# A two-layer fp32 decoder trunk on one core: the steps from each norm to the next matmuls in another order and in smaller pieces

## What is computed

```python
h = adaLN(RMSNorm(x), c)          # silu(c) @ ada_w + ada_b gives scale, shift and gate
x = x + gate1(c) * (hybrid_mixer(h) @ w_out)
h = adaLN(RMSNorm(x), c)
scores = sigmoid(h @ router_w); sel = scores + router_bias
grp_score = top_k(sel.reshape(ntok, 4, 4), 2)[0].sum(-1)   # sum of the two best of a group
best = argmax(grp_score)
for e in range(16):
    out += combine[:, e] * ((silu(h @ w_gate[e]) * (h @ w_up[e])) @ w_down[e])
x = x + gate2(c) * out
```

## Time and profile before

| | |
|---|---|
| median of 3 runs | 1483.7 us (1481.28 to 1484.05) |
| the profiled execution, its own time | 1478.49 us |
| its span in the profile | 1476.7 us |
| PE busy | 1408.2 us, 95% |
| DVE busy | 1159.0 us, 78% |
| ACT busy | 786.3 us, 53% |

### The profile page before, as it was taken

One profiled execution on the slowest core, in us unless ns is written; L12 is line 12 of the kernel. 1 busy time (PEld: TensorE's weight loads), 2 busy tenths in 40 slices (PEclk: granted clock), 3 DMA queues, 4 the chain that ended last, 5 costly groups with the idle time before them and its releaser, 6 DMA issues.

```text
span 1476.7 us, 19233 instructions
## 1 busy us (share of the span) xinstructions
PE 1408.2 (95%) x7638; PEld 1137.8 (77%) x7638; DVE 1159.0 (78%) x1344; ACT 786.3 (53%) x756; POOL 106.7 (7%) x180
## 2 busy tenths in 40 slices
PE   3999899999899999999989989999999999999998
PEld 3889777788799977766569877778879998776654
DVE  6589689865688878888875987898757856799886
...
DMA packets 174777, 357.46 MB, mean 242 GB/s; under 512 B 12316, under 2 KB 18704, under 8 KB 173664
## 3 DMA queue, kind: packets, MB, share of 16 engines
...
## 4 chain that ended last, share of the span: by engine, by line
PE 82%; DVE 9%; ACT 6%; issue 2%; DMA 1%; SPq 0%; DVEq 0%; ACTq 0%
PE bank L632 24%; PE bank L634 24%; PE bank L633 24%; DVE w_low L1718 4%; PE bank L1138 1%; PE bank L712 1%; DMA ring<-in_ada_w 1%; PE bank L596 1%; ACT w_high_zu L1240 1%; PE bank L760 1%; PE bank L807 1%; DVE scratch L2289 1%; PE bank L857 1%; PE bank L1035 1%; ACT w_high_xbc_sc L1217 1%
## 5 line engine op out<-in xcount | busy, mean ns | idle before, releaser
L634 PE MATMUL bank<-h_high,w_low 128*128 128x256 f32 x864 | 243.8, 282 | 0.0
L1718 DVE TENSOR_TENSOR w_low<-ring,w_high_qk_score 128x2048 fp32r<-128x2048 f32 x72 | 164.8, 2288 | 39.3 <-ACT w_high_qk_score L1217 21.3
L1718 DVE TENSOR_TENSOR w_low<-ring,w_high_zu 128x2048 fp32r<-128x2048 f32 x66 | 151.1, 2289 | 46.4 <-ACT w_high_zu L1240 26.4
L633 PE MATMUL bank<-w_low,h_high 128*128 128x512 f32 (+2 forms) x480 | 183.7, 383 | 0.0
L1718 DVE TENSOR_TENSOR w_low<-ring,w_high_xbc_sc 128x2048 fp32r<-128x2048 f32 x68 | 155.6, 2289 | 29.4 <-ACT w_high_xbc_sc L1217 27.1
L634 PEld LDWEIGHTS bank<-h_high,w_low 128*128 128x128 f32 x864 | 163.7, 189 | 0.0
L633 PE MATMUL bank<-w_low,rows_high 128*128 128x512 f32 (+2 forms) x384 | 151.6, 395 | 0.0
L1217 ACT ACTIVATE w_high_zu<-ring 128x2048 fp32r<-128x2048 f32 x50 | 95.6, 1911 | 69.9 <-PE bank L634 66.0
L1217 ACT ACTIVATE w_high_xbc_sc<-ring 128x2048 fp32r<-128x2048 f32 x50 | 95.6, 1912 | 62.0 <-PE bank L634 58.5
L1217 ACT ACTIVATE w_high_qk_score<-ring 128x2048 fp32r<-128x2048 f32 x52 | 99.5, 1913 | 32.4 <-PE bank L634 29.1
L633 PEld LDWEIGHTS bank<-w_low,h_high 128*128 128x128 f32 x480 | 91.5, 191 | 18.9 <-issue 1.9
...
## 6 DMA issues: line engine op xcount, KB each, us to landing
...
```

The costliest lines, as they stand in the source:

```text
L633: mm(out_, lh, rl, start=False, stop=False, skip_group_check=True)
L634: return mm(out_, ll, rh, start=False, stop=stop, skip_group_check=True)
L1718: V.tensor_tensor(w_low[:, slot, :, cols], ring[:, slot, :, cols], high[:, :, cols], ALU.subtract).then_inc(w_split, 1)
```

## The change

**Start of layer 0.** The two reciprocals and the scaling of tile 1 stand ahead of the seventh weighing. The last weighing is done in two column halves (`weigh_last`), and PE turns each half into columns as it is there. The fills ahead of the transposes are 4 instead of 8; the 5 ahead of the columns and the 8 behind them are replaced by 5 behind them. Unit 0 is rounded and split in two halves of the contraction (`start_rounded`, `start_split`), one ahead of the columns and one behind DVE's first modulation.

**Start of both layers.** The channel blocks are modulated in pairs: ACT takes blocks 0, 1 and 4, 5, DVE 2, 3 and 6, 7, and rounding and splitting go by the same pairs; the first projection waits pair by pair. In layer 1 two fills are added behind the transposes.

**Second norm to first expert, both layers.** Tile 0's modulation on DVE is cut in three blocks ahead of the last `add_output` and one behind; its rounding and splitting by halves; `xn_high` and `xn_low` by tile (`round_normed`, `split_normed`), the first tile's rounding inside the norm, the second's behind the sigmoid, the second's split behind the choice of groups. The sum of the two best of four is taken as the largest of two sums of pairs and one sum of the larger ones. Fills ahead of the counts are 3 instead of 6. Of the gathered rows, 4 and 6 on ACT and 5 and 7 on DVE are taken behind the pieces of the first expert unit.

The diff, cut to its core:

```diff
...
-            pe.wait_ge(sums_ready, layer + 1)
+            if layer > 0:
+                pe.wait_ge(sums_ready, layer + 1)
             for n in range(ADA_0):
+                if layer == 0 and n % 2 == 0:
+                    pe.wait_ge(first_columns, n // 2 + 1)
                 c0 = (MOE_CHUNKS - ADA_0 + n) * W
                 last = chunk_columns(bank[:, 3, :], PROWS + 4 * n, ada_sums[:, c0:c0 + W])
             last.then_inc(columns_in, 1)
...
             pe.wait_ge(first_used, 5)
-            busy(8)
+            busy(4)
         pe.wait_ge(xn_ready, l * 6 + 2)
         modulate_transposes(1)
         if l == 0:
-            pe.wait_ge(first_used, KD - 1)
+            layer_columns(0)
             busy(5)
-            layer_columns(0)
-            busy(8)
             pe.wait_ge(pcol_ready, 2)
+        else:
+            busy(2)
         b = begin("proj", "C")
         for h in range(2):
-            pe.wait_ge(h_split, l * 2 + h + 1)
             w = split_unit()
-            tok_project([b[:, 0, t * 256:t * 256 + 256] for t in range(TT)], w, h, 0, 256, h_early, True)
+            for k in (0, 2):
+                pe.wait_ge(h_split, l * 4 + 2 * h + k // 2 + 1)
+                tok_project([b[:, 0, t * 256:t * 256 + 256] for t in range(TT)], w, h, 0, 256, h_early, True,
+                            ks=range(k, k + 2))
             chan_project(b[:, 1:2, :], w, h, 256, range(2), h_early).then_inc(units_read, 1)
...
         b = begin("v", "count")
-        busy(6)
+        busy(3)
...
+            take_rows(4)
+            take_rows(6)
...
         def first_modulate():
+            def columns(b, k0):
+                for k in range(2):
+                    last = A(hT[:, k0 + k, :], b[:, k * SEQ:k * SEQ + SEQ], ACT.Identity,
+                             scale=modc[:, 0, 0, k0 + k:k0 + k + 1], bias=modc[:, 0, 1, k0 + k:k0 + k + 1])
+                last.then_inc(h_even, 1)
+            def rounded(k0):
+                A(h_high[:, k0:k0 + 2, :], hT[:, k0:k0 + 2, :], ACT.Copy).then_inc(h_rounded, 1)
             act.wait_ge(modc_ready, l * 2 + 1)
...
+            columns(job("s", "h1_0"), 0)
+            act.wait_ge(h_even, l * 2 + 1)
+            rounded(0)
+            act.wait_ge(h_odd, l * 2 + 1)
+            act.sem_inc(s_evac, 2)
+            seen["s"] += 1
+            rounded(2)
+            act.wait_ge(v_ready, l * NVR + V_PLAIN.index("h1_2") + 1)
+            columns(ps("h1_2"), 4)
+            act.wait_ge(h_even, l * 2 + 2)
+            rounded(4)
+            act.wait_ge(h_odd, l * 2 + 2)
+            act.sem_inc(v_evac, 2)
+            rounded(6)
+        def round_normed(t):
+            act.wait_ge(xn_ready, l * 6 + 4 + 2 * t)
+            A(xn_high[:, t, :], merged[:, t, :], ACT.Copy).then_inc(xn_rounded, 1)
...
-            round_mixer(0)
+            act.wait_ge(slot_loaded[0], 16 * LANDED[0])
+            for k in (0, 2):
+                A(mixer_high[0][:, k:k + 2, :], ring[:, 0, k:k + 2, :], ACT.Copy).then_inc(
+                    w_rounded if k else start_rounded, 1)
         first_modulate()
...
         second_square(0, 1)
         second_norm(0)
+        round_normed(0)
         second_square(1, 0)
         second_modulate(0)
+        act.wait_ge(s_evac, l * NSJ + S_JOBS.index("h2_0") + 1 + 2)
+        A(h2_high[:, 0:HK, 0:P], hT[:, 0:HK, 0:P], ACT.Copy).then_inc(h2_rounded, 1)
         second_square(1, 1)
         second_norm(1)
-        act.wait_ge(s_evac, l * NSJ + S_JOBS.index("h2_0") + 1 + 2)
         act.wait_ge(v_evac, l * NVJ + V_JOBS.index("h2_2") + 1 + 2)
-        A(h2_high[:, :, 0:P], hT[:, :, 0:P], ACT.Copy).then_inc(h2_rounded, 1)
+        A(h2_high[:, HK:, 0:P], hT[:, HK:, 0:P], ACT.Copy).then_inc(h2_rounded, 1)
...
-        act.wait_ge(xn_ready, l * 6 + 6)
-        A(xn_high[:, :, :], merged, ACT.Copy).then_inc(xn_rounded, 1)
...
+        round_normed(1)
+        def take_rows(k):
             b = job("s", f"rows{k}")
             A(rowsT[:, k, :], b[:, 0:ROWS], ACT.Identity, scale=modc[:, 1, 0, k:k + 1],
               bias=modc[:, 1, 1, k:k + 1]).then_inc(s_evac, 1)
+        take_rows(0)
+        take_rows(2)
...
+    def weigh_last():
+        acc = ada_sums[:, (MOE_CHUNKS - ADA_0) * W:]
+        dve.wait_ge(first_loaded[KD - 1], 16)
+        dve.wait_ge(first_used, KD - 1)
+        for h in range(2):
+            cols = slice(h * 2 * W, (h + 1) * 2 * W)
+            V.scalar_tensor_tensor(out=acc[:, cols], in0=first_w[KD - 1][:, cols], scalar=cact[:, KD - 1:KD],
+                                   in1=acc[:, cols], op0=ALU.mult, op1=ALU.add).then_inc(first_columns, 1)
+        dve.wait_ge(first_columns, 2)
+        dve.sem_inc(first_used, 1)
+        dve.sem_inc(sums_ready, 1)
...
+        def first_modulate(b, k0):
+            for k in range(2):
+                last = V.tensor_scalar(hT[:, k0 + k, :], b[:, k * SEQ:k * SEQ + SEQ],
+                                       modc[:, 0, 0, k0 + k:k0 + k + 1], modc[:, 0, 1, k0 + k:k0 + k + 1],
+                                       ALU.mult, ALU.add)
+            last.then_inc(h_odd, 1)
+        def split_start(ks):
+            return V.tensor_tensor(w_low[:, 0, ks, :], ring[:, 0, ks, :], mixer_high[0][:, ks, :], ALU.subtract)
+        def split_first(q):
+            dve.wait_ge(h_rounded, l * 4 + q + 1)
+            ks = slice(2 * q, 2 * q + 2)
+            V.tensor_tensor(h_low[:, ks, :], hT[:, ks, :], h_high[:, ks, :], ALU.subtract).then_inc(h_split, 1)
...
             weigh_first(KD - 3)
-            weigh_first(KD - 2)
         rstd(1, 0)
         rstd(1, 1)
         V.tensor_scalar(merged[:, 1, :], x_sb[:, 1, :], st[:, 2, 3:4], None, ALU.mult).then_inc(xn_ready, 1)
         if l == 0:
-            weigh_first(KD - 1)
-            dve.wait_ge(first_used, KD)
-            dve.sem_inc(sums_ready, 1)
-            split_mixer(0)
+            weigh_first(KD - 2)
+            weigh_last()
+            dve.wait_ge(start_rounded, 1)
+            split_start(slice(0, 2)).then_inc(start_split, 1)
             take_columns(0)
-        first_modulate()
-        for h in range(2):
-            hs = slice(HK * h, HK * h + HK)
-            dve.wait_ge(h_rounded, l * 2 + h + 1)
-            V.tensor_tensor(h_low[:, hs, :], hT[:, hs, :], h_high[:, hs, :], ALU.subtract).then_inc(h_split, 1)
+        dve.wait_ge(s_ready, l * NSJ + S_JOBS.index("h1_1") + 1)
+        first_modulate(ps("h1_1"), 2)
+        if l == 0:
+            dve.wait_ge(w_rounded, 1)
+            split_start(slice(2, HK)).then_inc(start_split, 1)
+            dve.wait_ge(start_split, 2)
+            dve.sem_inc(w_split, 1)
+        split_first(0)
+        split_first(1)
+        seen[0] += 1
+        first_modulate(job("h1_3"), 6)
+        split_first(2)
+        split_first(3)
...
         second_norm(0)
         add_output(1, 0)
         half_sums(1)
+        second_modulate(0, range(0, 3))
         add_output(1, 1)
-        second_modulate(0)
+        second_modulate(0, range(3, HK))
         second_norm(1)
-        split_second(0, slice(0, KD), slice(0, P))
+        for h in range(2):
+            split_second(h, slice(HK * h, HK * h + HK), slice(0, P))
         second_modulate(1)
         for h in range(2):
-            split_second(1 + h, slice(HK * h, HK * h + HK), slice(P, SEQ))
-        dve.wait_ge(xn_rounded, l + 1)
-        V.tensor_tensor(xn_low[:, :, :], merged, xn_high[:, :, :], ALU.subtract).then_inc(xn_split, 1)
+            split_second(2 + h, slice(HK * h, HK * h + HK), slice(P, SEQ))
+        def split_normed(t):
+            dve.wait_ge(xn_rounded, l * TT + t + 1)
+            V.tensor_tensor(xn_low[:, t, :], merged[:, t, :], xn_high[:, t, :], ALU.subtract).then_inc(xn_split, 1)
+        split_normed(0)
...
+        pair = rt1[:, 2, :, 0:3 * EG].rearrange("p t (g k) -> p t g k", g=EG)
+        top = rt1[:, 3, :, 0:2 * EG].rearrange("p t (g k) -> p t g k", g=EG)
+        op(top, G(1)[:, :, :, 0:2], G(1)[:, :, :, 2:4], ALU.max)
+        op(pair[:, :, :, 0:2], G(1)[:, :, :, 0:2], G(1)[:, :, :, 2:4], ALU.add)
+        settle()
+        op(pair[:, :, :, 2], top[:, :, :, 0], top[:, :, :, 1], ALU.add)
+        settle()
+        step(V.tensor_reduce(LG(4), pair, AX_X, ALU.max))
...
+        split_normed(1)
...
+        take_rows(1)
+        take_rows(3)
...
             split_piece(0, slice(k, k + 1), k + 1, w_split if k == HK - 1 else piece_split)
+        take_rows(5)
+        take_rows(7)
         split_piece(1, slice(0, 2), HK, piece_split)
```

52 lines of the change are left out of this document (11 added, 41 removed).

## The result

The changed kernel takes 1465.91 us (median of four runs, 1465.68 to 1468.31), the kernel before 1482.68 us (median of four, 1481.28 to 1484.05): ratio 0.9902 with a 95% interval of 0.9879 to 0.9924. The profiled executions are nearer to each other: 1466.03 against 1478.49, 12.5 us.

The account below looks back on a forecast made before the run. PE, busy for 95% of the span, was taken to bound the kernel. Savings of 4.0, 3.7, 1.2 and 2.2 us (11.1) took 1478.49 to 1467.4; 5.2 carried over gave 1472.6, range 1468.8 to 1478.3.

Parts of the forecast that it names:

- the carry-over: Whole kernel: the 5.2 us between the profiled execution of before and its runs' median was added to the forecast.
- my sum: Both starts and both ways from second norm to first expert: four savings adding up to -11.1 us.
- (e): Layer 0, ahead of the counts: six half-clock fills ended at 383.22, after the choice at 381.37; three would end early enough.
- Start of layer 0: Up to the first projection: PE starts 4.4 us earlier, then waits 0.4 for unit 1; net -4.0 us.
- the stand of 0.39: First projection: PE was to wait for unit 1, 0.4 us in layer 0 and 0.7 in layer 1.
- Start of layer 1: Up to the first projection: order by block pairs gives -1.9 us, unit 1 costs 0.7; net -1.2 us.
- The middle: Second norm to first expert: -3.7 us in layer 0 and -2.2 us in layer 1.
- term (c): Second norm to first expert: moving the rounding of normed rows brings the copy of the scores 2.3 us earlier.
- More than forecast: Rival: in layer 1 half clock leaves the router and unit 1 costs nothing; -13.5 us, 1470.2; chance 0.05.
- Half clock eats part of it: Rival: half clock also falls on layer 0's first projection and a gather of rows; +3.5 us, 1476.1; chance 0.17.

Follow-up runs that it names:

- starts_only: The kernel before with only the edits to the starts of the two layers: mean 1474.2 us, ratio 0.9961 to before.
- mid_only: The kernel before with only the edits from second norm to first expert, in both layers: mean 1473.1 us, ratio 0.9959 to before.
- fills_in_wait: The kernel before with four fills instead of one in PE's wait for the copy of the scores: mean 1478.9 us, ratio 0.9993 to before.
- fills3_alone: The kernel before with three fills instead of six ahead of the counts: mean 1482.5 us, ratio 1.0020 to before.
- fills_kept: The changed kernel with the fills of before put back at the starts and ahead of the counts: mean 1468.5 us, ratio 0.9930 to before.
- before_again: The kernel before, unchanged, run and profiled again: its profiled execution took 1475.27 us.

## Why the prediction was wrong

**The step that failed** is the carry-over, as I put it: "the runs shown have a median of 1483.7, 5.2 above it, and I carry the difference over". Two things were wrong in it. First, the 5.2 was mostly the draw of three runs: 81 runs have a median of 1480.0, 1.5 above that profiled execution. With 1480.0 as the base, my sum gives 1468.9, at the edge of the range and still 3 us above what came. Second, what lies between executions of before is time at half clock, and I treated it as a constant that the change would inherit. It is not: the changed kernel spends 28.4 us instead of 36.4 there, which is 4 of the 13.8 us between the means (Tc accounts for the other 9.8, less than my 11.1, since part of the half clock, that of (e) in layer 0, was inside my terms already). The first fault is shown by the 81 runs. That the fall in half clock makes up the 3 us that are left is argued from the clocks; the traces place only part of it.

**Right, by its own steps.** Start of layer 0 (-4.0; measured -3.6), with the columns, the modulation, PE's start and the stand of 0.39 for unit 1 each within 0.25. Start of layer 1 (-1.2; -1.4, the stand 0.38 instead of 0.7). The middle in layer 0 (-3.7; -3.8, and -3.6 up to the gather) and in layer 1 (-2.2; -2.5, and -2.1). starts_only and mid_only bear the split out: -5.7 and -6.8 for -5.2 and -5.9.

**Right by luck.** In layer 1, term (c) took 2.3 for the copy as in layer 0. But there PE waited only 0.35 for it, not 1.71, since its router matmuls stood at half clock. Had that stayed, the copy could have come only some 0.35 + 0.6 earlier (an estimate from these rows). It came 2.3 earlier because the half clock was gone, which the sum nowhere said.

**Right mechanism, wrong place in the order of likelihood.** *More than forecast* ("In layer 1 half clock no longer falls on the router and unit 1 costs nothing: -13.5, 1470.2") was given 0.05; the means came out at -13.8, though unit 1 did cost its 0.38, and though half clock on the router, which it wanted gone, had cost layer 1 nothing (14.83 us with it, 14.84 in fills_in_wait without). *Half clock eats part of it* was given 0.17, on the thought that fewer fills bring more of it. fills3_alone shows that thought true by itself (46.0 us). The stretch at half clock that the changed start has is no case of it, since fills_kept has it too (from 33.0), with the fills put back; it must come with another of the start's edits, and no run tells which. What I did not do was to set it against the wait that the change removes two microseconds earlier. The earlier trace rows had PE waiting 1.71 for the copy, had 0.50 right behind it in layer 0, and term (c) removed the wait.

The 14 traces have 28 middles. PE waits 1.7 for the copy in seven (layer 0 of before and of before_again, layer 1 of starts_only, both of fills3_alone and of rounding_late), and half clock follows in all seven. In three (the other layer of the first three) it came earlier, on the router's matmuls, behind the wait of 1.2 for h_low, and then hardly any wait for the copy was left. In the 18 middles of the nine traces in which a chain edit or fills closed the wait for the copy, there is none.

A rival stands beside this for the three: the change also shortened the wait for h_low, from 1.21 to 0.74. Half clock stands on the router in 3 of the 12 middles with 1.21 and in 0 of the 16 with 0.74. No run has that edit alone.

**Wrong in a detail.** I wrote that the six fills ahead of the counts cost where they ended late, and took the gain from cutting them. They ended late because they ran at half clock. At full clock six end in time (fills_kept: 12.72 us to the gather, as with three), so the gain came from the clock and not from the three fills. In the kernel before they also kept the half clock short.

**Not settled.** Where all of the 8.0 us at half clock went. The middles of before hold 6.8 of it in each trace and the changed start adds 3.4, so some 4.6 (an estimate) would have to be gone elsewhere, where nothing was edited; but there the two traces of before have 24 and 17 us of it and the two of after 24 each. Also open is why closing the wait with fills took away only half as much as closing it with the rounding (3.6 us a run against 8.1), though the traces of both have none in the middles. Each trace is one execution of many.
